# A hybrid decoder step on one core: w_in's columns in six pairs, with the delta rule's front and half its inverse between their tiles

## The chip, the cores and the metric

One core of a Trainium2 chip runs the whole program. The metric is the device time of one execution in microseconds (us). Below, PE is TensorE, DVE is VectorE, ACT is ScalarE, POOL is GpSimd, and SP is SyncE, which here only issues DMAs. All data is fp32. A fp32 weight product is made of three products of halves (a rounded part and its remainder), so every weight goes through a split first.

## What is computed

Two layers, D = 1024, over 256 prompt positions and 8 samples of one position each: 264 columns stand side by side everywhere. Each layer is

```python
x += 0.5 * post1(SwiGLU_1(pre1(x)))                  # 1024 -> 2816 -> 1024
x += post2(W_out concat[A, B, C, D](pre2(x)))        # heads fed by ONE input projection
x += 0.5 * post3(SwiGLU_2(pre3(x)))
# A dilated sliding-window attention   (q, k, v)      columns QA KA VA
# B forgetting attention, paged cache  (q, k, v, f)   columns QB VB KB, gates FB
# C gated delta rule                   (q, k, v, z, a, b)
#     q, k, v go through a 4-tap conv and SiLU; q, k are divided by their L2 norm per head
#     A_ij = (k_i beta_i) k_j exp(g_i - g_j), strictly lower;  T = inv(I + A)
#     v_new = T rhs;  out = q S + (q k^T * decay) v_new;  S = decay * S + k^T v_new
# D spatial gating                     (u, v)         columns UD VD
```

The 8 samples also attend to their own pasts: 8 pages of 128 cached positions each for B (read through a page table) and three windows for A, 11 tiles of 128x256 for the keys and 11 for the values of each sample. Each sample's delta state (16x1024) is read, updated and written.

## The kernel before, in words

There is no scheduler: each engine's program is written out by hand and runs in its order, and semaphores join them. A layer is six phases of weight products: gu1, dn1, wi (w_in), wo (w_out), gu2, dn2.

**Weights.** The weights of a phase come in pairs of tiles, s = 0 and 1, into two buffers. SP loads `raw`, ACT rounds it to `whi` (L591), DVE makes `wlo` = raw - whi (L888, helper `lo`), and PE runs three matmuls of 128x264 per 128 rows of the contraction (L1391, L1392, L1393, helper `three`). A wide tile is 256 columns: `wide_chunk` runs two halves of 24 matmuls, each into its own PSUM bank, and DVE scales them by the column norms into `proj` (helpers `take`, L985 to L1000). w_in has 7 pairs: six of 2 x 256 columns in the order of the matrix, and one narrow one for the rest.

**Between w_in and w_out.** PE turns `proj` to token-major (`tok`, `smp`) in 7 groups (L1504), then sums the gates with triangular constants (L1508 to L1513), turns the rows, builds decay terms from four-row operands (L1524, L1525), and runs the prompt's attention B (scores L1535, L1538, L1539; values L1566 to L1568), attention A, the spatial gating (L1644), and the delta rule: Gram products (L1657), transposes (L1665), and the triangular inverse in six levels, each a `y` product (L1678) and two products from it (L1687, L1688) with DVE work between (`lev`); after it new values (L1700), outputs (L1706) and the state (L1709). The conv of q, k, v is 7 tiles on DVE, each L1058 and three L1060.

**The samples.** SP reads the page table and issues each sample's keys into `kslot` (`keys`, L446, L435 to L437) and values into `vslot` (`vals`, L454). Samples use two slots in turn, so keys(b) waits until POOL used the slot (`k_used`), and vals(b) until PE did (`pv_mm`). POOL multiplies keys and queries (L855, L856, tile `prod`), DVE adds them up (L1114, L1116), ACT takes the exponent, and PE forms the values of two samples at a time (`sample_values`, L1590, L1592, four calls). The samples' own conv row `cv` is made on POOL and ACT, scaled on DVE (L1188, semaphore `s_conv`), and written to DRAM by SP (L513, `d_cn`), from where it comes back regrouped (`kq16`, `v64`) for the samples' delta state.

**The order that SP follows** after w_in's last matmul: keys and vals of samples 0 and 1 with the small stores between them, keys(2), keys(3), the gates' loads, eight output stores (L503 to L510), the wait for `s_conv` and L513, vals(2), vals(3), keys(4), keys(5), the eight loads of the states (L526), vals(4), vals(5), keys(6), keys(7), vals(6), vals(7). Page slots, `at_`, `qkt` and the other scratch lie in separate places of SBUF.

**The end of the stage.** `sample_values(3)`, the states' products, `so_mm` (L1733), DVE's normalisation of the samples' rows (L1340 to L1354), and PE's transposes of the mixed heads (L1740, L1741), behind which w_out's first matmul (L1391) stands.

## Time and profile before

| | us |
|---|---|
| median of 3 runs | 1602.6 (1593.21 to 1604.79) |
| the profiled execution | 1603.99 |
| its span | 1602.2 |
| w_in's last matmul starts, layer 0 | 314.73 |
| `s_conv` scale on DVE (L1188), layer 0 | 385.24 |
| last value page's issue, layer 0 | 483.01 |
| transposes of the mixed heads start, layer 0 | 546.62 |
| PE's mean granted clock over the span | 0.870 of 2.4 GHz |

How to read it: times of the trace count from the span's start. A row of the timeline is start, duration, engine, line, operation, output and inputs, shape and count, and in brackets how long the engine stood idle before it and on whom it waited. Rows with a count merge neighbours; their duration is from the first start to the last end. SPq is the queue that SP issues DMAs on, and its durations are those of issuing. Both layers run the same program, and layer 1 repeats layer 0 about 795 us later.

### The profile page before, as it was taken

What the parts mean: (1) busy time and instruction counts of PE and PEld (TensorE: products, weight loads), DVE (VectorE), ACT (ScalarE), POOL (GpSimd) and SP (SyncE); (2) the same over time, 40 slices, a digit from 0 to 9 for tenths busy, and PEclk for the clock granted to TensorE, in tenths of its full rate; (3) what the DMA queues carried; (4) which work ended last, traced back from release to release, by engine and by line L of the source; (5) the groups of instructions that cost most, each with busy time, mean ns of one, the idle gap of its engine ahead of it and who ended that gap; (6) DMA issues with size and microseconds to landing.
All of it is one profiled execution on the core that took longest, in us unless ns stands there. A gap on an engine that the chain in (4) does not pass through costs nothing.

```text
span 1602.2 us, 27946 instructions
## 1 busy us (share of the span) xinstructions
PE 1353.2 (84%) x9968; PEld 1257.8 (79%) x9968; DVE 944.8 (59%) x1508; ACT 652.6 (41%) x1054; POOL 216.7 (14%) x176
## 2 busy tenths in 40 slices
PE   6999979977587579999889999697866857699997
PEld 5999979966375369999889999697754735699996
DVE  4766355485654666664467654655756554666634
ACT  4655343343200255554456544434330004455543
POOL 1000010022332230000110000200323322200000
PEclk9999989967686589999989999899556966899998
DMA  6555554354461334555646556363444613255553
GB/s 213 183 184 160 163 177 131 96 155 138 147 192 49 93 105 134 184 172 162 182 129 190 172 155 181 106 199 97 129 130 138 185 38 106 83 184 183 159 168 94
DMA packets 286118, 234.15 MB, mean 146 GB/s; under 512 B 19898, under 2 KB 282018, under 8 KB 286056
## 3 DMA queue, kind: packets, MB, share of 16 engines
q1 hardware_dynamic: 286056, 233.37, 47.9%
q8 instruction: 33, 0.54, 0.1%
q14 instruction: 29, 0.24, 0.0%
HBM read 228.65 MB, written 5.37 MB: 146 GB/s over the span
## 4 chain that ended last, share of the span: by engine, by line
PE 76%; DVE 15%; ACT 3%; issue 3%; DMA 1%; SPq 0%; DVEq 0%; POOLq 0%; ACTq 0%
PE ps L1391 20%; PE ps L1392 19%; PE ps L1393 19%; PE ps L1590 2%; PE ps L1688 2%; DVE s L1114 2%; PE ps L1535 2%; DVE nlo L937 2%; PE ps L1687 1%; DVE yt L920 1%; PE ps L1538 1%; ACT whi L591 1%; PE ps L1504 1%; PE ps L1678 1%; PE ps L1733 1%
## 5 line engine op out<-in xcount | busy, mean ns | idle before, releaser
L1391 PE MATMUL ps<-nhi,whi 128*128 128x264 f32 x1936 | 564.2, 291 | 67.4 <-DVE nlo L937 47.0
L888 DVE TENSOR_TENSOR wlo<-raw,whi 128x1024 fp32r<-128x1024 f32 (+2 forms) x376 | 394.7, 1091 | 280.1 <-ACT whi L591 279.8
L1392 PE MATMUL ps<-nlo,whi 128*128 128x264 f32 x1936 | 558.5, 289 | 0.0
L1393 PE MATMUL ps<-nhi,wlo 128*128 128x264 f32 x1936 | 557.7, 288 | 0.0
L1391 PEld LDWEIGHTS ps<-nhi,whi 128*128 128x128 f32 x1936 | 375.2, 194 | 74.2 <-DVE nlo L937 35.9
L591 ACT ACTIVATE whi<-raw 128x1024 fp32r<-128x1024 f32 (+2 forms) x376 | 336.8, 945 | 190.9 <-PE ps L1393 113.4
L1392 PEld LDWEIGHTS ps<-nlo,whi 128*128 128x128 f32 x1936 | 375.4, 194 | 0.2
L1393 PEld LDWEIGHTS ps<-nhi,wlo 128*128 128x128 f32 x1936 | 373.2, 193 | 0.0
L1391 PE MATMUL ps<-hhi,whi 128*128 128x264 f32 x704 | 202.3, 287 | 9.1 <-DVE hlo L905 9.1
L1393 PE MATMUL ps<-hhi,wlo 128*128 128x264 f32 x704 | 201.4, 286 | 0.0
L1392 PE MATMUL ps<-hlo,whi 128*128 128x264 f32 x704 | 201.0, 286 | 0.0
L1391 PEld LDWEIGHTS ps<-hhi,whi 128*128 128x128 f32 x704 | 133.9, 190 | 9.9 <-issue 9.8
L1393 PEld LDWEIGHTS ps<-hhi,wlo 128*128 128x128 f32 x704 | 134.0, 190 | 0.0
L1392 PEld LDWEIGHTS ps<-hlo,whi 128*128 128x128 f32 x704 | 133.9, 190 | 0.0
L601 ACT ACTIVATE hhi<-h_t 128x264 f32 (+1 forms) x88 | 37.3, 424 | 172.7 <-DVE h_t L902 172.7
L813 POOL TENSOR_TENSOR ss_acc<-sq 128x264 f32<-128x264 f32 x12 | 10.0, 832 | 697.5 <-ACT sq L608 652.4
L816 POOL TENSOR_TENSOR ss_acc<-ss_acc,sq 128x264 f32<-128x264 f32 x72 | 60.8, 845 | 225.4 <-ACT sq L608 199.5
L855 POOL TENSOR_TENSOR prod<-kslot,q_bc 128x2048 f32<-128x2048 f32 x16 | 72.2, 4515 | 135.1 <-DVE s L1116 89.3
L905 DVE TENSOR_TENSOR hlo<-h_t,hhi 128x264 f32 (+1 forms) x88 | 38.2, 434 | 60.2 <-ACT hhi L601 60.2
L607 ACT ACTIVATE yt<-ps 128x264 f32 (+1 forms) x48 | 18.8, 391 | 92.9 <-PE ps L1393 92.9
L597 ACT ACTIVATE s_t<-s_t 128x264 f32<-128x264 f32 x88 | 36.3, 425 | 40.6 <-DVE s_t L895 40.3
L597 ACT ACT_TABLE_LOAD x40 | 51.3, 1283 | 0.7
(338 smaller groups left out, 1555.8 us busy)
## 6 DMA issues: line engine op xcount, KB each, us to landing
raw<-in_ffn_gate_dram SPq DMA_DIRECT2D x44, 1024.0 KB, 5.3
raw<-in_ffn_up_dram SPq DMA_DIRECT2D x44, 1024.0 KB, 5.4
raw<-in_ffn_down_dram SPq DMA_DIRECT2D x64, 704.0 KB, 4.5
raw<-in_w_in_dram SPq DMA_DIRECT2D x24, 1024.0 KB, 5.7
kslot<-in_cache_fox_k_dram SPq DMA_DIRECT2D x128, 128.0 KB, 2.7
vslot<-in_cache_fox_v_dram SPq DMA_DIRECT2D x128, 128.0 KB, 2.4
raw<-in_w_out_dram SPq DMA_DIRECT2D x8, 1024.0 KB, 5.1
kslot<-in_state_swa_k_dram SPq DMA_DIRECT2D x32, 128.0 KB, 2.7
```

What stands on the lines that cost most here:

```text
L591: act.activation(whi[s][:, a:b], raw[s][:, a:b], ACT.Copy).then_inc(S(f"w_hi{s}"), 1)
L597: act.activation(s_t[:, f, :], s_t[:, f, :], ACT.Silu).then_inc(S("silu"), 1)
L601: act.activation(hhi[:, bass.ds(2 * j + f, 1), :].rearrange("p o n -> p (o n)"), h_t[:, f, :], ACT.Copy).then_inc(S("h_hi"), 1)
L816: ins = tt_(ss_acc[:, :], ss_acc[:, :], sq8[:, t, :], ALU.add)
L855: tt_(prod[:, 0:NPG, :], kslot[:, i, 0:NPG, :], q_bc[:, i, GW:512].unsqueeze(1).broadcast_to([P, NPG, GW]), ALU.mult).then_inc(S("prod"), 1)
L888: tt2(wlo[s][:, a:b], raw[s][:, a:b], whi[s][:, a:b].bitcast(F32), ALU.subtract).then_inc(S(f"w_lo{s}"), 1)
L905: tt2(hlo[:, at, :].rearrange("p o n -> p (o n)"), h_t[:, f, :], hhi[:, at, :].rearrange("p o n -> p (o n)").bitcast(F32), ALU.subtract).t ...
L937: stt(nlo[:, t, :], x[:, t, :], gain(l + ahead, e, t), nhi[:, t, :].bitcast(F32), ALU.mult, ALU.subtract).then_inc(S("n_ready"), 1)
L1114: red(s13[:, u, 0:NPG, :], four_(prod[:, 0:NPG, :]), AX.X, ALU.add).then_inc(S("s_red"), 1)
L1391: mm(out, wh, hi_, start=first, stop=False)
L1392: mm(out, wh, lo_, start=False, stop=False)
L1393: return mm(out, wl, hi_, start=False, stop=last)
```

## The change

It does five things in each layer.

1. w_in's columns are regrouped into six pairs of wide tiles in the order C's q, k, v, then B's, A's, D's and z; the twelve gate columns come apart as a tile of 128x224 (`graw`), loaded by two DMAs of 4 and 8 columns a row, split by ACT and DVE, and multiplied in 24 matmuls ahead of pair 1. Wide matmuls: 24 tiles of 24 instead of 25.
2. After each half of pairs 1 to 5, PE runs a piece of what used to stand behind w_in: gates, sums, norms, decay broadcasts, Gram products, transposes, levels 0 to 2 of the inverse, and the token-major transposes. Levels 3 to 5 stand behind w_in, between attention B's pieces, and the new values, outputs and state of the delta rule stand between attention B and attention A.
3. The delta rule's front is rewritten: L2 norms and gates are added as logarithms and go in with one exponent; decays come from a broadcast and one DVE operation a head, written straight to `at_` and `qkt`; the conv of v's two tiles is on POOL (14 operations), that of q and k on DVE; POOL makes `wlo` for s = 1 of pairs 2 to 5.
4. The page slots `kslot` and `vslot` lie in the weight buffers; `at_`, `qkt`, `tt`, `tm`, `ys`, `kd` lie where `kslot` was, and `prod`, `q_bc` and others where `vslot` was. keys(0) waits for the last `wlo` of w_in, and all other pages for w_in's last matmul.
5. SP's order: keys(1), vals(0), vals(1), the eight output stores and the states' loads, then the wait for `s_conv`; keys(2) and keys(3) stand behind it. On DVE the `s_conv` scale stands behind the second new values of the delta rule. The samples' state work stands between the later samples' reductions instead of at the end.

```diff
+WCOL = ((QC, QC + GW), (QC + 2 * GW, QB_), (KB_, VB_), (QA, KA), (VA, VD), (UD, ZC))
...
+        w_at = here[0]
...
+        kslot = place("kslot", [P, 2, NKT, GW], at=w_at)
+        vslot = place("vslot", [P, 2, NKT, GW + 1], at=w_at + 8 * NKT * GW)
...
# SP
+                    for s in range(2):
+                        sp.wait_ge(S(f"w_lo{s}"), V(f"w_lo{s}", 2 * (P0["wi"] + WI_P)))
+                    keys(0)
...
                     for s in range(2):
                         sp.wait_ge(S(f"mm_done{s}"), V(f"mm_done{s}", M0["wo"]))
-                    sp.wait_ge(S("slot_zero"), V("slot_zero", 4))
-                    keys(0)
-                    vals(0)
...
-                    for b in (2, 3):
-                        keys(b)
...
                     sp.wait_ge(S("s_conv"), V("s_conv", 1))
                     sp.dma_start(d_cn.rearrange("c b (h e) -> (c b h) e", h=H), cv[:, 8, :]).then_inc(S("regroup"), 16)
+                    for b in (2, 3):
+                        keys(b)
...
# DVE
-                    sample_shift(0)
-                    dve.wait_ge(S("mix_r"), V("mix_r", 1))
-                    ts(cv[:, 8, :], cv[:, 8, :], small[0:96, 0:1], C("q_scale", 96), ALU.mult, ALU.mult).then_inc(S("s_conv"), 1)
...
+                    tt2(kb_n[:, 0, :], vb[:, 1, :], kb_n[:, 0, :], ALU.subtract).then_inc(S("rhs1"), 1)
+                    sample_shift(0)
+                    dve.wait_ge(S("vn_mm"), V("vn_mm", 2))
+                    dve.tensor_copy(vn[:, 1, :], ps[:, 5, 0:GW]).then_inc(S("vn"), 1)
+                    dve.wait_ge(S("mix_r"), V("mix_r", 1))
+                    ts(cv[:, 8, :], cv[:, 8, :], small[0:96, 0:1], C("q_scale", 96), ALU.mult, ALU.mult).then_inc(S("s_conv"), 1)
...
# PE
+                    def beside(j, s, i):
...
+                        elif (j, s, i) == (1, 1, 0):
+                            cumulate()
+                        elif (j, s, i) == (1, 1, 1):
+                            head_norms()
...
+                        elif (j, s) == (2, 1):
+                            broadcast(i)
+                        elif (j, s) == (3, 0):
+                            gram(i)
...
+                        elif (j, s, i) == (4, 1, 1):
+                            pe.wait_ge(S("tok_act"), V("tok_act", SMP_AT[3] + 1))
+                            level_z(0)
```

On PE the first of the new places is in w_in's second pair. Before, one half follows the other there; a stretch of the program before, at the end of w_in and into what follows it:

```order
L1393 MATMUL ps<-nhi,wlo_78 128x264
L1504 MATMUL ps<-const,proj 128x128 [waits pd_taken,pa_taken]
L1504 MATMUL ps<-const,proj 128x128 x7
...
L1504 MATMUL ps<-const,proj 8x128
L1508 MATMUL ps<-gate,const 128x8 [waits gate_act]
L1509 MATMUL ps<-gate,const 128x4
```

The program after, at the first half of pair 1's tile s = 1 (L1453 to L1455 are the three matmuls, L1573 to L1578 are L1508 to L1513 of before):

```order
L1455 MATMUL ps<-nhi,wlo_83 128x264
L1573 MATMUL ps<-gate,const 128x8 [waits gate_dve]
L1574 MATMUL ps<-gate,const 128x4
...
L1578 MATMUL ps<-gate,const 128x4
L1453 MATMUL ps<-nhi,whi_81 128x264 [waits pd_taken]
L1454 MATMUL ps<-nlo,whi_81 128x264
```

The gates' sums moved from behind all of w_in into the middle of its second pair, and the matmuls of the next half stand behind their wait.

On SP, around the wait for `s_conv`, before:

```order
L446 DMA kslot<-in_cache_fox_k_dram 128x256
L435 DMA kslot<-in_state_swa_k_dram 128x256
...
L501 DMA gb<-d_gate 32x2 [waits gb_pre]
...
L510 DMA out_swa_k_sample_dram<-smp 8x256
L513 DMA d_cn<-cv 96x64 [waits s_conv]
L454 DMA vslot<-in_cache_fox_v_dram 128x256 [waits pv_mm]
```

and after:

```order
L525 DMA out_swa_v_prompt_dram<-tok 128x2x256
L527 DMA proj<-in_state_gdn_s_dram 16x1024 x8
L531 DMA d_cn<-cv 96x64 [waits s_conv]
L470 TENSOR_LOAD ptab
...
L498 DMA q_bc<-d_q 128x512 [waits k_used0]
L486 ISA
L486 DMA kslot<-in_cache_fox_k_dram 128x256
```

Six samples' keys and values, instead of four samples' keys and six samples' values, stand behind that wait.

On DVE, ahead of the instruction that raises `s_conv`, before:

```order
L1101 COPY ptr<-ps 128x512 [waits p_turned]
L1103 RECIPROCAL small<-small 128x8 [waits p_exp]
L1105 TENSOR_TENSOR otok<-ps,small 128x2x256 [waits o_mm,dve_ch]
L1139 TENSOR_TENSOR s_119<-s_119,pmax_all 128x2x36 [waits s_max_all]
L1140 TENSOR_TENSOR s_119<-s_119,pmax_all 128x2x16
L1188 TENSOR_SCALAR cv<-cv,small,const 96x64 [waits mix_r]
```

and after, where `lf_turned`, `vn_mm`, `oc_mm` and `ks_mm` are raised by PE behind the inverse's levels and `scores(1)`'s matmuls:

```order
L1232 TENSOR_REDUCE s_124<-prod 128x12 [waits k_used0]
L1156 TENSOR_TENSOR tt<-tt,ps 128x4x64 [waits tm_act,z_mm0]
L1156 TENSOR_TENSOR tt<-tt,ps 128x4x64 [waits tm_act,z_mm1]
L1290 COPY ptr<-ps 128x256 [waits lf_turned]
...
L1232 TENSOR_REDUCE s_124<-prod 128x12 [waits k_used1]
L1296 COPY vn<-ps 128x256 [waits vn_mm]
...
L1318 TENSOR_TENSOR kb_n<-vb,kb_n 128x256
L1255 TENSOR_TENSOR s_124<-s_124,pmax_all 128x2x36 [waits s_max_all]
L1256 TENSOR_TENSOR s_124<-s_124,pmax_all 128x2x16
L1321 COPY vn<-ps 128x256 [waits vn_mm]
L1323 TENSOR_SCALAR cv<-cv,small,const 96x64 [waits mix_r]
```

The instruction that raises `s_conv` moved from behind attention B's first half to behind the whole inverse and both chunks' new values.

## Rows read from the trace of the kernel before

**Rows 1.** The page: the chain that ended last, by engine.

```profile
PE 76%; DVE 15%; ACT 3%; issue 3%; DMA 1%; SPq 0%; DVEq 0%; POOLq 0%; ACTq 0%
```

**Rows 2.** Windows: length; busy PE, PEld, DVE, ACT, POOL; PEclk, DMA share, GB/s.

```profile
252.00:315.10 63.10, 61.26 (x505) 60.97 (x504) 34.17 (x49) 19.54 (x22) 0.00 (x0) 1.00 0.46 144
...
330.00:385.50 55.50, 47.61 (x199) 39.87 (x200) 38.16 (x73) 19.14 (x43) 15.69 (x12) 0.59 0.50 153
385.50:483.50 98.00, 71.24 (x496) 55.64 (x495) 57.73 (x104) 14.28 (x34) 36.36 (x13) 0.74 0.53 160
```

**Rows 3.** Timeline of SP's queue, layer 0.

```profile
321.38 3.99 SPq L446 DMA_DIRECT2D kslot<-in_cache_fox_k_dram  x8
...
362.33 0.37 SPq L458 DMA_DIRECT2D q_bc<-d_q  x1
...
373.25 0.33 SPq L458 DMA_DIRECT2D q_bc<-d_q  x1
...
395.19 3.70 SPq L454 DMA_DIRECT2D vslot<-in_cache_fox_v_dram  x8
...
400.48 3.85 SPq L454 DMA_DIRECT2D vslot<-in_cache_fox_v_dram  x8
...
483.01 0.49 SPq L437 DMA_DIRECT2D vslot<-in_state_swa_v_dram  x1
```

**Rows 4.** Waits of SP's queue, both layers: total us, times, longest.

```profile
SPq L454 <- PE ps L1592: 17.5, 2, 9.0
```

**Rows 5.** Timeline: `s_conv` on DVE, and the end of the stage on PE.

```profile
385.24 0.30 DVE L1188 TENSOR_SCALAR cv<-cv,small,const 96x64 f32<-96x64 f32 x1
...
509.53 3.60 PE L1590 MATMUL ps<-vslot,s 128*4 128x257 f32 x28
...
531.55 6.43 PE L1733 MATMUL ps<-oms,const 100*8 100x256 f32 x16
546.62 0.66 PE L1740 MATMUL ps<-const,otok 128*128 128x128 f32 x2 [8.64 <-DVE smp_o L1354]
```

**Rows 6.** Timeline of PE: w_in's start and end, transposes, products of the inverse.

```profile
235.65 0.56 PE L1391 MATMUL ps<-nhi,whi 128*128 128x264 f32 x1 [7.49 <-DVE nlo L937]
...
236.23 0.42 PE L1393 MATMUL ps<-nhi,wlo 128*128 128x264 f32 x1
...
314.73 0.28 PE L1393 MATMUL ps<-nhi,wlo 128*128 128x264 f32 x1
315.53 8.41 PE L1504 MATMUL ps<-const,proj 128*128 128x128 f32 x75 [0.53 <-DVE proj L1000]
...
448.31 2.17 PE L1678 MATMUL ps<-tm,at__84 128*128 128x128 f32 x16
...
461.66 0.39 PE L1687 MATMUL ps<-ys,tt 128*128 128x128 f32 x2
461.89 0.39 PE L1688 MATMUL ps<-tt,ys 128*128 128x128 f32 x2
```

**Rows 7.** Timeline of ACT: the gates' chain.

```profile
325.32 0.23 ACT L676 ACTIVATE gate_t<-gate_in 128x36 f32<-128x36 f32 x1 [0.96 <-DVE gate_in L1017]
...
328.40 0.23 ACT L678 ACTIVATE gate_t<-gate_t 128x36 f32<-128x36 f32 x1
```

**Rows 8.** Timeline of DVE and POOL where a conv meets a product.

```profile
331.22 1.52 DVE L1060 SCALAR_TENSOR_TENSOR conv_t<-proj,cwt,conv_t 128x255 f32<-128x255 f32 x3
...
338.84 7.70 DVE L1060 SCALAR_TENSOR_TENSOR conv_t<-proj,cwt,conv_t 128x255 f32<-128x255 f32 x3
...
339.99 4.50 POOL L855 TENSOR_TENSOR prod<-kslot,q_bc 128x2048 f32<-128x2048 f32 x1
```

**Rows 9.** Timeline of PE: `scores(0)` from its first matmul to the next piece.

```profile
343.81 0.79 PE L1535 MATMUL ps<-proj 64*128 64x128 f32 x2
...
366.21 3.25 PE L1549 MATMUL ps<-const,conv_t 128*128 128x128 f32 x14
```

**Rows 10.** The page: DMA queue: packets, MB, share of 16 engines.

```profile
q1 hardware_dynamic: 286056, 233.37, 47.9%
```

More of the change, by code:

```diff
@@ L117, in constants @@
     put("eps", np.full((P, 1), EPS))
+    put("eps64", np.full((P, 1), HD * EPS))
+    put("half", (i[:, None] // HD == np.arange(2)[None, :]))
     scale = np.ones((P, 1))
@@ L243, in build @@
+        conv_t = place("conv_t", [P, NCT, L])
+        vb = place("vb", [P, 2, GW])
+        here[0] = max(here[0], f_at + 8 * FT * N + 16 * N)
         f_end = here[0]
@@ new lines, in _ @@
+                    h8 = lambda ap: ap.rearrange("p t (h i) -> p (t h) i", h=H)
+                    h22 = lambda ap: ap.rearrange("p (b a i) -> p a b i", b=2, a=2)
+                    four = lambda ap: ap.rearrange("p t (h d) -> p t h d", h=H)
+                    wide = lambda name: C(name).unsqueeze(1).broadcast_to([P, 8, P])
+                    for i in range(2):
+                        take(0, 0, i)
+                    lo("wi", 1, 0)
+                    for i in range(2):
+                        take(0, 1, i)
@@ new lines, in _ @@
+                    lo("wi", 1, 1)
+                    dve.wait_ge(S("gates_mm"), V("gates_mm", 1))
+                    tt2(proj[0:12, NPT - 1, :], ps[0:12, 4, 0:N], r_pre[0:12], ALU.mult).then_inc(S("gates_taken"), 1)
+                    dve.wait_ge(S("par_taken"), V("par_taken", 3))
+                    dve.wait_ge(S("pd_taken"), V("pd_taken", 4))
+                    for t in range(4):
+                        conv(t)
+                    for i in range(2):
+                        take(1, 0, i)
@@ new lines, in _ @@
+                    lo("wi", 2, 0)
+                    dve.wait_ge(S("gate_act"), V("gate_act", 1))
+                    ch(stt(gate[:, :, :], gate_in[:, :, :], 0.0, gate_t[:, :, :], ALU.max, ALU.add))
+                    tt2(gate[:, :, :], gate[:, :, :], mul12[:, :].unsqueeze(1).broadcast_to([P, 3, 12]), ALU.mult).then_inc(S("gate_dve"), 1)
+                    for i in range(2):
+                        take(1, 1, i)
+                    dve.wait_ge(S("gate_mm"), V("gate_mm", 1))
+                    dve.tensor_copy(cum[:, :], ps[:, 7, 40:64]).then_inc(S("cum_sb"), 1)
@@ new lines, in _ @@
+                    ch(stt(ex[:, :, 2, :], lk, -0.5, cg, ALU.mult, ALU.subtract))
+                    dve.tensor_copy(ex[:, :, 4, :], lnb)
+                    dve.tensor_copy(ex[:, :, 5, :], tot)
+                    tt2(ex[:, :, 0, :], ex[:, :, 0, :], lnb, ALU.add)
+                    tt2(ex[:, :, 3, :], ex[:, :, 2, :], tot, ALU.add).then_inc(S("ex"), 1)
+                    for i in range(2):
+                        take(2, 0, i)
+                    lo("wi", 3, 0)
+                    dve.wait_ge(S("gate_mm"), V("gate_mm", 2))
@@ new lines, in update @@
+                    def update(k):
+                        last = k == len(LEVELS) - 1
+                        part = lambda ap, side: ap.rearrange("p (c a e) -> p c a e", a=2, e=LEVELS[k])[:, :, side, :]
+                        for t in range(NT):
+                            dve.wait_ge(S(f"z_mm{t}"), V(f"z_mm{t}", k + 1))
+                            dve.wait_ge(S("tm_act"), V("tm_act", 2))
+                            if not last:
+                                tt2(part(tm[:, t, :], 0), part(tm[:, t, :], 0), part(ps[:, 4 + 2 * t, :], 0), ALU.subtract)
+                            tt2(part(tt[:, t, :], 1), part(tt[:, t, :], 1), part(ps[:, 5 + t if last else 5 + 2 * t, :], 1), ALU.subtract).then_inc(S(f"lev{t}"), 1)
@@ L1083, in _ @@
[L1083 to L1089 removed]
+                    masked_y(0)
@@ new lines, in level_z @@
+                    def level_z(k):
+                        last = k == len(LEVELS) - 1
+                        for t in range(NT):
+                            pe.wait_ge(S(f"ys{t}"), V(f"ys{t}", k + 1))
+                            for h in range(H):
+                                if not last:
+                                    mm(ps[:, 4 + 2 * t, hp(h)], tt[:, t, hp(h)], ys[:, t, hp(h)], start=True, stop=True)
+                                ins = mm(ps[:, 5 + t if last else 5 + 2 * t, hp(h)], ys[:, t, hp(h)], tt[:, t, hp(h)], start=True, stop=True)
+                            ins.then_inc(S(f"z_mm{t}"), 1)
```

1058 lines of the change are left out of this document (562 added, 496 removed).

## The prediction

> **What bounds the kernel now.** I read the page's chain first, then windows of the stretch that the change touches, then SP's queue in it, then single instructions. The chain is PE for 76% [rows 1], mostly weight products, and these the change leaves alone. The windows show two different halves [rows 2]. In w_in PE is busy 61.26 of 63.1 us at the full clock (505 matmuls, 0.121 each), with DVE at 34.17, ACT at 19.54 and POOL at nothing: there is room beside it on those engines, none on PE. Behind w_in PE is busy 71.24 of 98 us at 0.74, so something else leads there. It is SP's queue [rows 3]: keys of one sample follow those of another after 10.9 us (362.33 to 373.25), values after 5.3 (395.19 to 400.48), from 321.38 to 483.5. In that stretch it waits little: its longest wait is 9.0 us for `pv_mm` [rows 4], and `s_conv`, raised at 385.24 [rows 5], comes as SP reaches it. The end is PE again: `sample_values(3)` starts at 509.53, though its pages were issued by 483.5, and the transposes of the mixed heads start at 546.62 [rows 5]. I call w_in's end T_w (315.0 [rows 6]) and `s_conv`'s scale T_s (385.24 [rows 5], T_w + 70.2). From T_s to the transposes it is 161.4 us.
>
> **First part: w_in's stretch.** The wide matmuls are as many as before, 600 a layer. The pieces between them add to PE, at full clock: some 60 transposes at 0.112 (8.41 / 75 [rows 6]) 6.7; gates' sums 2.7 (L1508 to L1513, 330.21 to 332.9); Gram products 2.3 (L1657); the inverse's 8 transposes 0.9; three y levels at 2.2 and three z levels at 16 x 0.22 (461.66 to 461.89 [rows 6]) 3.6, 17.2; small ones 1.3. Sum 31. None of it is hidden: PE was full here.
>
> Then PE's in-order waits. The gates' sums stand in pair 1 and wait for the gates; behind them stands half of w_in. The gates need their matmuls, a transpose, ACT's chain of 3.3 us with two table loads (325.32 to 328.63 [rows 7]) behind a `whi` pair of 2, and a DVE step that stands behind the four convs of q and k, 4 x (0.35 + 1.52) = 7.4 [rows 8]. I schedule it: PE reaches the wait at 265.1, the gates come at 275.2: 10 us idle (bounds 3, if the convs finished early, and 12). The decay rows cost 2.9 by the same method, the first z level 1.8, other waits 1. Then the clock: after 7.49 us idle w_in's own third matmul takes 0.42 and not 0.28 [rows 6], and such matmuls start 0.22 apart for 4.6 us; that is 2 us. The narrow seventh pair and its waits go, -2. So T_w moves by 31 + 15.7 = 47, to 362. Bounds: +31 to +4 of waits (350), and 370.
>
> The gate columns' DMAs have packets of 16 and 32 bytes, 2048 a layer. A packet takes 0.479 x 16 x 1602 / 286056 = 43 ns [rows 10]; over 16 engines that is 5.5 us of queue beside gu1's weights, or nothing if it finds a gap. I take 0 (bounds 0 and 5.5).
>
> **Second part: from T_w to T_s.** Before, 70.2 us, in which `scores(0)` took 22.4 (343.81 to 366.21 [rows 9]) at half clock. Now DVE's `s_conv` scale stands behind the whole inverse, attention B's values and the second new values. In PE's order: z of level 2 3.6, y3 with its waits 2.9, transposes 1.8, z3 3.6, own samples' rows on DVE and y4 4.1, `scores(0)` 17.7 (between 22.4 at half clock and 11.2 at full; above the middle, since its four-row matmuls ran at half clock to the last [rows 9]), z4 5.7, the turn of q and k and y5 4.4, then DVE's mask, the reductions of the first sample and `lf_sb` 10.2, the decays' sums 4.6, new values 1.9, turn of p 2.0, outputs and state 2.6, values 4.5, the state's product 2.0, `scores(1)` 3.5, new values 1.9. Sum 77.0, so T_s = 439. Bounds: 57 with all of it at full clock and nothing blocked, 86 with all at half.
>
> In this sum 8 us are for one thing the trace shows: three convs' DVE operations that take 1.52 elsewhere take 7.70 when they meet POOL's 4.50-us product of keys [rows 8]. After the change products of samples 0 and 1 stand beside DVE's own-row work and `lf_sb`, on which PE waits: 3.2 + 5. The Trainium skill (SBUF — State Buffer, "Who interferes with whom") says that VectorE and GpSimd share a port pair, and that a VectorE operation with two SBUF inputs waits for a whole GpSimd instruction. By that rule, the trace agrees: the conv has two such inputs. The rule also speaks against putting v's conv and `wlo` on POOL beside DVE's convs in w_in's stretch; without it my sum would be 8 us a layer lower.
>
> **Third part: from T_s to the end.** SP has nothing to issue from about T_w + 35, when both slots are full, until T_s, since six samples stand behind the wait. Then it issues d_cn 0.4, keys(2, 3) 21.8, `kq16` and `v64` 3.5, vals(2, 3) 10.6, keys(4, 5) 21.6, vals(4, 5) 11.7, keys(6, 7) 21.0, a store 0.6, vals(6, 7) 12.0: 103.2 by the steps of [rows 3] (before, 98.3 from T_s with two waits of 9.0 and 3.4 in them and two samples' keys fewer). The last lands 2.7 later, and ACT's exponent for it stands behind the mix's norms: T_s + 109. Then `sample_values(3)` 6.6, its division 0.9, `so_mm` 6.4 [rows 5], and DVE's 8.6 [rows 5]: the transposes at T_s + 131. Before, 161.4: the samples' state chain (516.2 to 531.5) no longer stands behind `sample_values(3)`, and neither do the inverse and the new values, which held its start to 509.53. So this part gains 30.4. At full clock it is T_s + 126.
>
> **The sum.** A layer: +47 + 6.8 - 30.4 = +23.4. Two layers: +46.8. On the profiled execution, 1603.99, that makes 1650.8; the median of the runs lies 1.4 below, so 1649. What was hidden before (delta rule beside SP's pages) now stands in front of `s_conv`, which lets the pages go; that outweighs the shorter end.
>
> **Rivals.**
> *PE never idles (faster).* The place is the gates' sums: if DVE serves the gates before the convs end, the stall is 3 us or less, and a PE that does not idle keeps the full clock that w_in has in [rows 2] through the levels and `scores(0)`. Then T_w = 350, T_s = 407, transposes 533: -13.6 a layer, -27.2 in all, 1575. Against it: DVE's order puts the convs ahead, and the clock stayed at 0.59 through the four-row matmuls [rows 2], which remain. It decides for faster once T_s comes before 416 in layer 0. Chance 0.13.
> *Stall as forecast, then full clock (no change).* T_w 362, T_s 362 + 57 to 65, end +126: 545 to 553 against 546.6, -1.6 to +6.4 a layer, 1599 to 1615. For it: behind w_in there is now denser PE work than before. Chance 0.15.
> *More of the same (slower still).* POOL's 14 conv operations and 8 `wlo` halt DVE in w_in, T_w 362 to 370; at half clock T_s is 84 to 86 later and the transposes 132 behind that: 578 to 588, +31 to +41 a layer, 1665 to 1684. For it: a DVE operation of 0.48 became one of 6.6 in [rows 8]. Chance 0.25, and the packets of the gates' DMAs are in it.
> *The change does not do what it says*, since the pieces stand between the tiles but hide nothing, PE being full there: that is the forecast's own ground, and has no chance of its own.
>
> **How the numbers follow.** The forecast itself, 1620 to 1664, holds 0.47. The range must leave out 2 in 10: its low end is 1595, which lets out most of the first rival; its high end 1690, above the third. A measurement of this kernel tells about 1% from no change (its runs spread by 0.7%), 1586.6 to 1618.6. Faster 0.13; within 1% 0.15; slower 0.72.
>
> **What would show it.** In the trace after: w_in's last matmul near 362 in layer 0 (350 to 370), with one idle of some 10 us before L1573; a PEclk under 0.8 in the 77 us behind it; no page issued in the 35 to 40 us before `s_conv` at about 439; a `sample_values(3)` some 109 us behind that, bound by its pages; the mixed heads' transposes 5 to 10 us nearer to the last page. Wrong if T_s comes before 416, if PE does not wait at L1573, or if DVE shows no operation stretched by a POOL product.

## The result, and the profile after

The kernel after takes 1700.98 us (median of 4 runs, 1699.47 to 1702.37), the kernel before 1600.32 beside it (1593.21 to 1604.79): a ratio of 1.0635, interval 1.060 to 1.067. The forecast was 1649.0, range 1595 to 1690. The direction was right, the size was not: the time lies above the range, 52 us over the forecast. The profiled execution took 1702.08, its span 1700.3. Medians and ratios are those of fast runs: one execution below, 2044.35 us at a granted clock of 0.62 in the squares' run, was slow and is left out.

The page's chain that ended last (shares of the span of 1700.3 us):

```profile
PE 64%; DVE 13%; SPq 9%; issue 7%; ACT 4%; DMA 1%; POOL 1%; POOLq 0%; DVEq 0%; ACTq 0%
```

Against [rows 1], PE's share of the chain fell from 76% to 64%. SP's queue, which stood at 0%, has 9% now, and "issue", time in which an engine waited for nothing that the profile shows, went from 3% to 7%. Those two entries are where to look.

Windows of layer 0 (length; busy PE, PEld, DVE, ACT, POOL with instructions; granted clock, DMA share, GB/s). They are cut at w_in's end, at `scores(0)`, at `s_conv`, at the last pages, and at the transposes of the mixed heads:

```profile
250.00:367.80 117.80, 102.08 (x749) 97.50 (x749) 56.17 (x126) 40.18 (x55) 34.50 (x29) 0.88 0.27 79
367.80:385.00 17.20, 11.74 (x100) 11.11 (x99) 12.18 (x18) 4.38 (x8) 7.83 (x8) 0.95 0.50 150
385.00:410.60 25.60, 25.60 (x89) 20.00 (x87) 1.87 (x5) 0.00 (x0) 0.00 (x0) 0.50 0.59 177
410.60:451.60 41.00, 31.19 (x203) 29.22 (x202) 23.25 (x40) 13.38 (x29) 6.85 (x3) 0.75 0.00 1
451.60:558.00 106.40, 32.89 (x228) 18.44 (x228) 51.39 (x83) 9.84 (x26) 38.95 (x15) 0.60 0.58 172
558.00:598.40 40.40, 12.25 (x68) 3.44 (x68) 9.85 (x18) 9.00 (x12) 13.65 (x8) 0.58 0.20 66
```

Read the last column first. From 410.6 to 451.6 the DMA engines carry 1 GB/s: nothing is in the queue. From 451.6 to 558 they carry 172, and PE is busy 32.89 of 106.4 us: it mostly waits for the samples' pages and what hangs on them. From 558 to 598.4 neither is busy, and no engine passes 14 of 40 us: a chain of short steps. Before, [rows 2] has PE busy 71.24 of 98 us in the stretch with the pages.

The three places are in the timelines. SP's queue (start, duration, line, operation), where "x8" are the eight pages of one sample:

```profile
400.07 3.73 SPq L527 DMA_DIRECT2D proj<-in_state_gdn_s_dram  x8
...
451.94 0.31 SPq L531 DMA_DIRECT2D d_cn<-cv  x1
...
457.46 4.36 SPq L486 DMA_DIRECT2D kslot<-in_cache_fox_k_dram  x8
...
548.90 3.95 SPq L494 DMA_DIRECT2D vslot<-in_cache_fox_v_dram  x8
```

The queue stands idle from 403.8 to 451.9, 48.1 us, as long as `s_conv` isn't raised (DVE's scale is at 451.62). PE, at the places where it waits or changes its pace:

```profile
273.29 0.59 PE L1573 MATMUL ps<-gate,const 128*128 128x8 f32 x2 [9.81 <-DVE gate L1081]
...
367.71 0.28 PE L1455 MATMUL ps<-nhi,wlo 128*128 128x264 f32 x1
...
384.50 3.75 PE L1656 MATMUL ps<-tm,at__88 128*128 128x128 f32 x16 [4.52 <-DVE tt L1156]
...
429.60 1.22 PE L1807 MATMUL ps<-ptr,const 128*128 128x256 f32 x2 [6.55 <-DVE ptr L1291]
...
576.57 3.60 PE L1780 MATMUL ps<-vslot,s 128*4 128x257 f32 x28 [42.85 <-ACT s L764]
...
598.44 0.66 PE L1878 MATMUL ps<-const,otok 128*128 128x128 f32 x2 [8.64 <-DVE smp_o L1416]
```

So T_w is 367.8 instead of 315.0 (+52.8), T_s is 451.6 instead of 385.24, and the transposes start at 598.44 instead of 546.62 [rows 5]: +51.8 in this layer. The last piece of the chain, read in order of time, holds the largest single surprise (start, length, engine, tile, line):

```profile
557.39 0.39 POOL pmax_all L906
...
557.87 11.58 issue
569.44 1.88 POOL tm L915
571.33 1.87 POOL tt L915
...
573.22 1.23 DVE small L1396
...
574.47 0.32 ACT small L781
...
576.11 0.23 ACT small L782
576.34 0.19 ACT s L764
```

POOL's all-reduce for the last two samples is done at 557.8, and DVE has the exponent's input ready at 558.15. The exponent (L764) runs at 576.3. On ACT it stands behind the mixed heads' norms (L781, L782), which need DVE's reductions (L1396) of squares that POOL makes (L915), and POOL begins them 11.6 us after its all-reduce.

### The profile page after: what moved, and what is told of

Same layout as the page of the kernel before. It is cut to its first block, busy times and chain, and to the rows that moved or that the text cites. A ratio compares the mean times of both kernels' runs of the same rounds, so it can differ in the third digit from the quotient of the medians.

```text
span 1700.3 us, 27532 instructions
## 1 busy us (share of the span) xinstructions
PE 1335.2 (79%) x9902; PEld 1238.7 (73%) x9902; DVE 898.9 (53%) x1450; ACT 656.4 (39%) x1048; POOL 275.5 (16%) x219
## 4 chain that ended last, share of the span: by engine, by line
PE 64%; DVE 13%; SPq 9%; issue 7%; ACT 4%; DMA 1%; POOL 1%; POOLq 0%; DVEq 0%; ACTq 0%
PE ps L1453 17%; PE ps L1454 17%; PE ps L1455 17%; SPq L470 2%; SPq L486 2%; DVE wlo L938 2%; ACT whi L605 2%; SPq L494 2%; DVE nlo L987 1%; PE ps L1735 1%; PE ps L1656 1%; DVE yt L970 1%; PE ps L1665 1%; PE ps L1738 1%; PE ps L1666 1%
## 5 line engine op out<-in xcount | busy, mean ns | idle before, releaser
L1453 PE MATMUL ps<-nhi,whi 128*128 128x264 f32 x1920 | 569.1, 296 | 63.5 <-DVE nlo L987 46.4
L1455 PE MATMUL ps<-nhi,wlo 128*128 128x264 f32 x1920 | 559.2, 291 | 0.0
L938 DVE TENSOR_TENSOR wlo<-raw,whi 128x1024 fp32r<-128x1024 f32 (+1 forms) x352 | 373.9, 1104 | 295.0 <-ACT whi L605 295.0
L1453 PEld LDWEIGHTS ps<-nhi,whi 128*128 128x128 f32 x1920 | 379.0, 197 | 72.8 <-DVE nlo L987 34.2
L605 ACT ACTIVATE whi<-raw 128x1024 fp32r<-128x1024 f32 (+1 forms) x368 | 333.8, 956 | 169.7 <-PE ps L1455 102.7
L1454 PEld LDWEIGHTS ps<-nlo,whi 128*128 128x128 f32 x1920 | 379.2, 197 | 0.2
L1455 PEld LDWEIGHTS ps<-nhi,wlo 128*128 128x128 f32 x1920 | 376.5, 196 | 0.0
L1453 PE MATMUL ps<-hhi,whi 128*128 128x264 f32 x704 | 201.1, 286 | 9.1 <-DVE hlo L955 9.1
L1455 PE MATMUL ps<-hhi,wlo 128*128 128x264 f32 x704 | 200.0, 284 | 0.0
L1453 PEld LDWEIGHTS ps<-hhi,whi 128*128 128x128 f32 x704 | 132.4, 188 | 10.2 <-issue 9.9
L1455 PEld LDWEIGHTS ps<-hhi,wlo 128*128 128x128 f32 x704 | 132.7, 188 | 0.0
L1780 PE MATMUL ps<-vslot,s 128*4 128x257 f32 x352 | 46.6, 546 | 107.3 <-ACT s L764 107.3
L1780 PEld LDWEIGHTS ps<-vslot,s 128*4 128x4 f32 x352 | 13.6, 107 | 135.1 <-ACT s L764 107.9
L1230 DVE TENSOR_REDUCE s<-prod 128x32 f32<-128x2048 f32 x16 | 36.5, 2281 | 85.9 <-POOL prod L902 85.9
```

The lines of the kernel that those rows point to most:

```text
L605: act.activation(whi[s][:, a:b], raw[s][:, a:b], ACT.Copy).then_inc(S(f"w_hi{s}"), 1)
L938: tt2(wlo[s][:, a:b], raw[s][:, a:b], whi[s][:, a:b].bitcast(F32), ALU.subtract).then_inc(S(f"w_lo{s}"), 1)
L1230: red(s13[:, u, 0:NPG, :], four_(prod[:, 0:NPG, :]), AX.X, ALU.add).then_inc(S("s_red"), 1)
L1453: mm(out, wh, hi_, start=first, stop=False)
L1454: mm(out, wh, lo_, start=False, stop=False)
L1455: return mm(out, wl, hi_, start=False, stop=last)
```

## The experiments

The theory after reading the trace: orders make the loss, and three of them hold PE (pages behind `s_conv`, the last exponent behind the squares, the gates' sums in w_in). The rival: a length of work that no order takes away (w_in's pieces, SP's pages, the half clock). Each run is compared with the kernel before; the kernel after stands at 1.0635. "A layer" is half the difference in ratio, at 1600 us. All but one are variants of the kernel after, and their line numbers differ from its own by up to three.

**The last exponent first.**

```diff
# ACT
                     sample_exp(2)
+                    sample_exp(3)
                     act.wait_ge(S("mix_ss"), V("mix_ss", 3))
...
-                    sample_exp(3)
```

> The changed kernel, with ACT's exponent for the last two samples (sample_exp(3)) put ahead of the mixing norms' Ln and Exp instead of behind them. Theory: in the changed kernel the last value product waits 42.85 us for that exponent, of which 18 us (558.2, when DVE has its input ready, to 576.2) are only ACT's order; with the order undone the product starts near 559, and then the mixing on POOL, which ends at 586.6, becomes the last one: transposes at about 588 instead of 598.4, 10 us a layer, 1701 - 21 = 1680 us. Rival (the last pages bind there): the order is covered and nothing moves, 1701.

1694.74, ratio 1.0601 (1.0565 to 1.0636), 3 us a layer; the interval overlaps that of the kernel after. In the profiled execution, the fastest of the four, the transposes start at 592.34, 6.1 sooner. PE at the end of the stage:

```profile
558.16 3.59 PE L1780 MATMUL ps<-vslot,s 128*4 128x257 f32 x28 [24.90 <-ACT s L764]
...
574.95 6.53 PE L1871 MATMUL ps<-oms,const 100*8 100x256 f32 x16 [7.76 <-DVE oms L1265]
```

`sample_values(3)` did start 18.4 us sooner (558.16 for 576.57), as expected. But its division on DVE (L1263 to L1265) stands behind the same reductions of the squares, so a part of the gain went back into a wait of PE for `oms` (7.76), and another into the one for `smp_o` (10.86 for 8.64). One wait was hidden behind another for the same release.

**The squares ahead of the last all-reduce.**

```diff
# POOL, sample 7
                         tt_(prod[...], kslot[...], ...).then_inc(S(f"k_used{i}"), 1)
+                        if b == B - 1:
+                            for t in range(NT): tt_(squares[t], otok[:, t, :], otok[:, t, :], ALU.mult).then_inc(S("o_sq"), 1)
                         if i == 1:
                             pool.partition_all_reduce(...)
```

> The changed kernel, with POOL's two squares of the mixed heads put ahead of its last all-reduce instead of behind it (they need nothing of it); ACT and DVE as changed. In the changed kernel POOL starts them 11.7 us after that all-reduce has ended, with nothing that the profile shows to wait for, and with the exponent put ahead the end came only 6 us a layer earlier, because DVE's last division stood behind the same squares. Theory (the 11.7 us follow every all-reduce on POOL and stand in the chain of the last samples): the squares run before 556, the exponent follows at 563 instead of 576, transposes 11 to 13 us a layer earlier, 1701 - 24 = 1677; the gap then shows ahead of the mixing (L920) instead. Rival (the gap belongs to the squares' inputs): it moves with them, under 4 us a layer.

1680.26 (3 runs), ratio 1.0554 (1.0505 to 1.0602), 6.5 us a layer, where 12 were expected; the transposes start at 589.19, 9.2 sooner. On POOL:

```profile
552.05 1.89 POOL L911 TENSOR_TENSOR tm<-otok 128x1024 f32<-128x1024 f32 x1
...
561.96 0.39 POOL L914 PARTITION_ALL_REDUCE pmax_all<-pmax  x1 [6.17 <-issue]
571.18 1.89 POOL L921 TENSOR_TENSOR otok<-otok,small 128x1024 f32<-128x1024 f32 x1 [8.83 <-issue]
```

The squares now follow the product without a gap. The idle time did not go with them: it stands ahead of what comes after the all-reduce, here the mixing (L921). ACT gave the mixing its norm at 566.88, so of the 8.83 us the last 4.3 have no input to wait for. So idle time follows the all-reduce and not the squares; that all 11.6 us of the kernel after belong to it is not shown. The all-reduce itself started 4.6 us later, with the squares ahead of it.

**Keys 2 and 3 ahead of the wait for `s_conv`.**

```diff
# SP
+                    for b in (2, 3):
+                        keys(b)
                     sp.wait_ge(S("s_conv"), V("s_conv", 1))
                     sp.dma_start(d_cn..., cv[:, 8, :])
-                    for b in (2, 3):
-                        keys(b)
```

> The changed kernel, with keys(2) and keys(3) issued by SP ahead of the wait for s_conv, as the kernel before did. Theory (SP stands idle from 404 to 452 while it has pages to issue): keys(2) goes at 404, keys(3) after k_used1 at 431, and behind s_conv stand 22 us less; the next wait is pv_mm for vals(2), near 460, so about 16 us a layer come off the last page, 1701 - 32 = 1669. Rival (the pages did not bind, or POOL's product of sample 2 now halts DVE ahead of s_conv): under 8 us a layer, over 1685.

1669.24, ratio 1.0440 (1.0393 to 1.0486), 15.6 us a layer, as expected. SP's queue and the transposes:

```profile
410.35 4.34 SPq L486 DMA_DIRECT2D kslot<-in_cache_fox_k_dram  x8
...
433.07 4.02 SPq L486 DMA_DIRECT2D kslot<-in_cache_fox_k_dram  x8
...
462.96 3.68 SPq L494 DMA_DIRECT2D vslot<-in_cache_fox_v_dram  x8
```

```profile
582.55 0.66 PE L1878 MATMUL ps<-const,otok 128*128 128x128 f32 x2 [8.64 <-DVE smp_o L1416]
```

Keys 2 go out 47 us sooner, but keys 3 only when POOL has used its slot, and vals 2 only when `sample_values(0)` has (462.96 for 477.36). Of 20 us of keys taken off the end (457.46 to vals 2 at 477.36), 15.9 are gained.

**`s_conv` itself early.**

```diff
# DVE: squares of cv behind update(3), the scale ahead of update(4)
                     update(3)
+                    ch(tt2(cv[0:64, 7, :], cv[0:64, 8, :], cv[0:64, 8, :], ALU.mult))
+                    red(small[0:64, 0:1], cv[0:64, 7, :], AX.X, ALU.add).then_inc(S("mix_ss"), 1)
...
+                    ts(cv[:, 8, :], cv[:, 8, :], small[0:96, 0:1], C("q_scale", 96), ALU.mult, ALU.mult).then_inc(S("s_conv"), 1)
                     update(4)
# ACT: the two small activations between ahead of the copies of q and k
```

> The changed kernel, with the samples' conv norm and scale made early: DVE's squares behind level 3's update, ACT's Ln and Exp behind the gates' SiLU, DVE's scale (s_conv) ahead of level 4's update; SP's order as changed. Theory (s_conv's place holds the pages): s_conv comes near 390 instead of 452, SP then issues keys(2) at 404 and keys(3) after k_used1 at 431, vals(2) after pv_mm near 460: the same 16 us a layer as with the keys ahead of the wait, 1669. If the wait for s_conv were only one of several that end together, under 5 us a layer, over 1690.

1666.32, ratio 1.0407 (1.0373 to 1.0441), 18 us a layer. The scale ran at 391.66, and the rest follows the run above to within 2 us:

```profile
405.80 0.42 SPq L531 DMA_DIRECT2D d_cn<-cv  x1
...
464.45 3.68 SPq L494 DMA_DIRECT2D vslot<-in_cache_fox_v_dram  x8
```

Two different edits, one in SP's order and one in DVE's, give the same time within their intervals. So it is keys 2 and 3 behind `s_conv` that cost, and once these are free, the values of samples 0 and 1 lead.

**The gates' sums half a tile later.**

```diff
# PE
-                        elif (j, s, i) == (1, 1, 0):
-                            cumulate()
                         elif (j, s, i) == (1, 1, 1):
+                            cumulate()
                             head_norms()
```

> The changed kernel, with the gates' cumulative sums on PE moved one half of a tile later (behind the second half of pair 1's s = 1 instead of the first). Theory: of PE's 9.8 us of waiting for the gates 5.8 are then filled with 24 matmuls, and the half clock behind the wait gets shorter: 6 to 8 us a layer off the end of w_in, and as much off the end, 1701 - 14 = 1687. Rival (what comes off there is given back behind w_in, where SP and POOL set the pace): under 2 us a layer, over 1697.

1694.23, ratio 1.0580 (1.0548 to 1.0613), 4.4 us a layer, with an interval that overlaps that of the kernel after.

```profile
274.80 0.60 PE L1573 MATMUL ps<-gate,const 128*128 128x8 f32 x2 [6.89 <-DVE gate L1081]
```

The wait fell by 2.9 us to 6.89, where 4 were expected to be left of it. w_in ended 1.8 sooner (365.88), but `s_conv` came at 451.82, no sooner than before the edit: from 433 to 447 the granted clock was 0.62 here and 0.74 in the kernel after, with PE busy 12.6 of 14 us in both. PE still was 1.7 us ahead at `lf_sb`'s products (427.90 for 429.60), so what was won in w_in was lost behind them, and the clock is what the rows show to differ there. The transposes did start 2.6 sooner.

**All five orders, then the samples' sums too.** The first run has the five edits above together. The second also puts `sample_add(0)` and `sample_add(1)`, DVE's sums of products, ahead of `update(4)` on DVE.

> The changed kernel with the orders put right together: s_conv early, keys(2) and keys(3) ahead of its wait, the squares ahead of the last all-reduce, the last exponent ahead of the norms, the gates' sums half a tile later. Theory (pages 14.5 us a layer, the last exponent 12, the sums 1 to 2, and they add up): 28 us a layer, 1701 - 56 = 1645. Rival (they cover each other): as the better of them alone, 1666. Neither reaches 1600: w_in's end, 52 us later than before, and the pages behind it stay.

> As the run with all orders, and DVE's reductions of samples 0 and 1 moved from behind the mask of attention B into DVE's 25 us of idle time beside scores(0), which lets POOL make sample 1's product there instead of beside lf_sb. Theory (in the changed kernel POOL's product at 424.8 halted DVE's L1291 for 4.04 us, PE waited 6.55, and two reductions of 3.2 stood ahead of it): the first value product comes 8 to 10 us a layer earlier, and with it vals(2), which wait for it: 1645 - 17 = 1628. Rival (SP's own pace): under 3 us a layer, over 1639.

1640.91, ratio 1.0291 (1.0262 to 1.0320), and 1619.16, ratio 1.0166 (1.0130 to 1.0203). The five single gains, with `s_conv` counted once, add up to 0.0034 + 0.0081 + 0.0228 + 0.0055 = 0.040; together they gave 0.0344. Each of these ratios is known to some 0.0035, so the sum and the run agree, and whether the exponent and the squares cover each other is not shown. The sums of the samples are worth 10 us a layer: they release POOL's product of the next key pair and with it PE's wait for `ptr` (6.55), which fell to 1.17. Still 1.7% above the kernel before, with all three orders of the theory undone, so they were not the whole.

**POOL's product behind level 3.** On top of the last kernel, POOL's first product waits until DVE has done level 3.

```diff
# POOL
                         if b:
                             pool.wait_ge(S("s_red"), V("s_red", 2 * b))
+                        else:
+                            for u in range(NT):
+                                pool.wait_ge(S(f"lev{u}"), V(f"lev{u}", 4))
                         tt_(prod[:, 0:NPG, :], ...
```

> As the run with the samples' sums early, and POOL's product of sample 0 waits for level 3 of the inverse, so that it no longer stands beside DVE's own-row work (L1273 took 3.93 us there, and PE waited 4.6 for level 3). Two theories of the half clock in scores(0), 0.50 for 25 us: (a) PE's 4.6 us of waiting just ahead lowers it; then without that wait scores(0) takes 11 to 13 us instead of 22.4, and 3.5 + 10 us a layer come off: 1619 - 27 = 1592. (b) The four-row and 64-row matmuls of scores(0) themselves keep it low: then only the wait goes, 3 to 4 us a layer: 1619 - 7 = 1612, with scores(0) still at 22 us or falling to it after its first us.

1601.66 (10 runs), ratio 1.0018 (0.9990 to 1.0047): 12 us a layer more, and the time of the kernel before. PE goes into `scores(0)` without the wait of 4.5 us and at the full clock, and then:

```profile
377.86 2.02 PE L1659 MATMUL ps<-tm,at__88 128*128 128x128 f32 x16 [0.94 <-DVE tt L1160]
379.81 0.48 PE L1737 MATMUL ps<-proj 64*128 64x128 f32 x2
...
382.96 0.48 PE L1737 MATMUL ps<-proj 64*128 64x128 f32 x2
...
384.17 0.79 PE L1737 MATMUL ps<-proj 64*128 64x128 f32 x2
```

A group of six matmuls (two on 64 rows, four on 4) takes 1.05 us three times (379.81 to 382.96), once 1.21, then 1.87 (384.17 to 386.04) eight times. No idle time stands between; in a window from 384.2 to 399.1 PE is busy all of 14.9 us at a granted clock of 0.50. The full clock fell while PE was busy throughout, in matmuls on 64 and on 4 rows. `scores(0)` took 19.3 us, and from 399.1 to 430 the clock was 0.92. The transposes of the mixed heads start at 546.56; before, 546.62 [rows 5].

Not all of this gain is the product beside DVE's own-row work. PE reaches the product behind `lf_sb` at 413.57 for 421.18, 7.6 us sooner. Another 4.5 us come at the end of the stage, where the edit did nothing but shift the times: in the 1.0166 kernel (1614.47 in its profile) DVE's squares of the samples' rows (L1408) ran beside POOL's mixing, took 1.83, 2.08 and 2.11 us, and PE waited 13.18 for `smp_o`; here the mixing ends before them, they take 0.68, 0.40 and 0.40, and the wait is 8.64.

```profile
545.94 1.83 DVE L1408 TENSOR_TENSOR ptr<-smp_o 8x512 f32<-8x512 f32 x1
...
558.36 0.66 PE L1877 MATMUL ps<-const,otok 128*128 128x128 f32 x2 [13.18 <-DVE smp_o L1416]
```

In layer 1 the wait fell from 12.76 to 8.76, but the matmuls ahead of it took 2.9 us longer, and the profiled layer as a whole gained nothing (the transposes there start 11.05 sooner, 11.8 of it from layer 0). So a part of the 12 us is luck in how two engines' times fall.

**Without the four-row matmuls.** The same kernel but the one before this (1.0166), with the four-row matmuls of `scores(0)` left out; the forget terms of attention B are not computed.

```diff
# PE
-                                ins = mm(o, qh[...], kh[...], start=True, stop=(m == 1))
-                                if m == 0:
-                                    mm(o, rows[:, 0, ...], hr(h), start=False, stop=False)
-                                    ins = mm(o, hr(h), rows[:, 1, ...], start=False, stop=True)
+                                ins = mm(o, qh[...], kh[...], start=True, stop=True)
```

> As the run with the samples' sums early, but scores(0) leaves out its 24 four-row matmuls of 36 (the forget gates' terms are missing from attention B of the prompt, so this is a measurement and no variant). By (b) of the run before this one, if the four-row matmuls hold the clock down, the 12 left run at full clock after a few us: under 2.5 us in all, 20 us a layer. If 64-row matmuls hold it too, they take 7.5 us (12 of 36 at the same rate), 15 us a layer. The end gains less than that where SP's pages set the pace: vals(2) wait for the first value product, so 12 to 15 us of it should show a layer: 1619 - 27 = 1592.

1596.29 (10 runs), ratio 0.9988 (0.9962 to 1.0014), 14 us a layer where `scores(0)` fell from 22.4 to 2.70:

```profile
384.32 2.70 PE L1734 MATMUL ps<-proj 64*128 64x128 f32 x24
...
398.23 1.94 PE L1789 MATMUL ps<-const,tok 128*128 128x128 f32 x8 [7.45 <-DVE tt L1157]
```

The granted clock is 0.50 at their start (384.3 to 385.0), 0.53 to 386.0, and 1.00 from there, so the 24 matmuls on 64 rows did not keep it down. Nor is the clock the whole price. The 24 on 64 rows of `scores(1)`, with nothing between them, take 3.46 us at 0.50 in this run, and 1.92 in the run before:

```profile
421.00 3.46 PE L1734 MATMUL ps<-proj 64*128 64x128 f32 x24
```

At the same half clock `scores(0)` with its 48 on 4 rows between them takes 22.4 us, and two matmuls on 64 rows there take 0.72 us from start to start (0.36 each for 0.144). At the full clock its twelve groups, at 1.05 each, would be 12.6 (an estimate). So the clock is worth some 10 us of the 22.4, and the four-row matmuls with what they do to their neighbours some 11 even at the full clock; why a neighbour gets slower stays open. Part of what is won comes back as a wait of 7.45 for DVE, whose sums of sample 1 now stand ahead of level 4 and wait for POOL's product.

**The remainders of the weights back on DVE.** The 1.0166 kernel with `wlo` for s = 1 on DVE and not on POOL.

```diff
# POOL
-                    for j in range(2, WI_P):
-                        lo("wi", j, 1)
# DVE, between the pieces of w_in
+                    lo("wi", 2, 1)
...
```

> As the run with the samples' sums early, with the weights' remainders (wlo) of s = 1, pairs 2 to 5, made by DVE again and not by POOL (2.35 us a pair instead of 4.7, and no POOL reads beside DVE there; in the changed kernel DVE's L1092 took 2.00 and L938 2.88 beside POOL). Theory: DVE has 62 us of idle time in w_in's 118, the remainders come 2 to 4 us sooner, nothing is gained or lost where PE did not wait for them: within 3 us of 1619. Rival (POOL was taken for this with reason): DVE's rows, masks and levels come later and PE waits, over 2 us a layer: over 1624.

1619.43, ratio 1.0166 (1.0098 to 1.0235): no difference. From 250 to 367.8 DVE is busy 64.14 us and POOL 16.05, where the kernel after has 56.17 and 34.50. w_in ended at 369.20 and not at 364.73, and the transposes at 564.61 and not at 558.36; but in layer 1 the transposes start 3.9 sooner (1345.84 for 1349.77), so no gain or loss of the order shows. The interval leaves room for some 6 us a layer either way: POOL's part in w_in is not where the 50 us a layer went.

**The kernel before, with the samples' state work between.** One idea of the change by itself, in another place: the states' steps leave the end of the stage and stand between levels 3 to 5 and the new values. In the kernel after they stand between the later samples' reductions (L1373 to L1390). All else is as before.

```diff
# DVE, kernel before
+                    beside = {3: decayed, 4: summed, 5: differed}
...
+                        if k in beside:
+                            beside[k]()
...
-                    ch(ts(state[:, :, :], state[:, :, :], eb[:, 0:1], None, ALU.mult))
-                    ch(tt2(sk, state[:, :, :], kc16, ALU.mult))
-                    red(sk_r[:, :], sk.rearrange("p k v -> p v k"), AX.X, ALU.add).then_inc(S("sk"), 1)
# PE: the first state product behind level 4, the second behind ks_mm; ACT: sg ahead of sample_exp(3)
```

> The kernel before, with one thing of the change alone: the samples' state update is no longer done behind the last value product, but its DVE steps one by one between the inverse's levels 3 to 5 and the new values, its two sums on PE there too (skp and sk_r lie in free places of proj). Theory (in the kernel before 15.3 us of that chain stand behind sample_values(3), and DVE idles beside each level): 8 to 13 us a layer, 1600 - 21 = 1579. Rival (the steps lie on the chain of the levels, which sets sample_values(3)): within 4 us a layer of 1600, or above it.

1574.45 (6 runs, 1569.25 to 1586.14), ratio 0.9877 (0.9841 to 0.9914): 10 us a layer, and faster than both kernels. Its end of the stage on PE, against [rows 5]:

```profile
520.14 3.62 PE L1746 MATMUL ps<-oms,const 100*8 100x256 f32 x16 [0.98 <-DVE oms L1149]
537.61 0.66 PE L1753 MATMUL ps<-const,otok 128*128 128x128 f32 x2 [13.86 <-DVE smp_o L1363]
```

`so_mm` starts 11.4 us sooner, the transposes 9.0. The wait for `smp_o` is 13.86 instead of 8.64, and DVE and POOL of that stretch say why:

```profile
524.51 2.24 DVE L1355 TENSOR_TENSOR ptr<-smp_o 8x512 f32<-8x512 f32 x1
...
532.43 2.92 DVE L1361 TENSOR_TENSOR smp_o<-smp_o,small 8x1024 f32<-8x1024 f32 x1 [1.90 <-ACT small L764]
```

```profile
524.31 1.90 POOL L870 TENSOR_TENSOR otok<-otok,small 128x1024 f32<-128x1024 f32 x1 [7.26 <-ACT small L757]
```

DVE's normalisation of the samples' rows now meets POOL's mixing: 2.24 us for an operation that took 0.68 in the kernel before, 2.92 for one that took 1.21. It is the collision of the 1.0166 kernel again.

## Why the prediction was wrong in size

**The first part, w_in: +52.8, forecast +47.** The idle time at L1573 is 9.81 (said 10), and the waits from 250 on 15.7, as forecast. Added up from their starts, the pieces take 31.5 us (said 31). The step that failed is the clock: "w_in's own third matmul takes 0.42 ... that is 2 us". The 600 matmuls on weights, the gates' 24 with them, take 85.4 us from w_in's start, and before 75.7: 9.7 more, not 2. (w_in also starts 1.1 us sooner, which hides a part; the sums are good to about 1 us.) Such matmuls start 0.22 apart and not 0.12 in four places behind the gates: behind the wait to 281, at 284 to 288, and behind each of the two broadcasts with four-row operands (L1611), 302 to 305 and 308 to 311, the last of them with no idle time ahead. The forecast had priced one such place. The granted clock was 0.56 to 282, 0.88 to 296, 0.69 to 310, and 0.99 only from there:

```profile
273.20:282.00 8.80, 8.00 (x37) 7.83 (x37) 0.90 (x4) 1.98 (x3) 5.41 (x7) 0.56 0.40 121
...
296.00:310.00 14.00, 12.04 (x49) 10.17 (x50) 6.63 (x22) 3.63 (x4) 2.52 (x2) 0.69 0.26 76
310.00:367.80 57.80, 55.22 (x457) 53.65 (x457) 25.59 (x57) 14.88 (x20) 13.82 (x12) 0.99 0.24 70
```

**The second part, T_w to T_s: +83.8, forecast +77.0 (before, 70.2).** The step that failed is "`scores(0)` 17.7", a middle between 22.4 and 11.2. It took 22.4, from 388.18 to 410.58, all of it at 0.50 (in layer 1 it took 20.0, its first three groups at the pace of the full clock). The run with the product moved makes 17.7 look out of reach: even entered at the full clock with no idle time, `scores(0)` takes 19.3. [rows 9] had the right price, and I moved away from it towards a clock that no row showed in these matmuls. That is 4.7 of the 6.8 us. The blocks of DVE by POOL's product were of the size forecast: the waits are 4.52 and 6.55 (forecast 3.2 and 5; in the repaired kernels 0.94 and 1.17 are left of them without a block). Some 1 to 2 us of this part stay without a row of their own. On DVE:

```profile
376.94 3.93 DVE L1273 TENSOR_SCALAR small<-small 8x8 f32<-8x8 f32 x1
...
425.50 4.04 DVE L1291 TENSOR_TENSOR ptr<-const,gate 8x256 f32<-8x256 f32 x1
```

POOL's products of 4.60 and 4.51 us start at 376.25 and 424.76. The second row has two inputs in SBUF, as the rule that the prediction cited wants, and takes 0.40 where no product stands beside it. The first, on 8x8 elements, has one, and takes 0.16 elsewhere. The Trainium skill (SBUF — State Buffer, "Who interferes with whom") also says that copies and `tensor_scalar` can enter modes that take both ports and then contend with GpSimd. The trace agrees in time, with 3.93 us for 64 elements, though no row shows the mode.

**The third part, T_s to the transposes: 146.8, forecast 131.** This is over half of the miss. SP's pages took 102.4 us behind T_s by the trace (forecast 103.2), and the exponent's input was ready at T_s + 106.5 (forecast + 109). The step that failed is the sentence "ACT's exponent for it stands behind the mix's norms: T_s + 109": I named the wait and priced it at the 3 us between 103.2 + 2.7 and 109. The wait is worth 18: 11.6 on POOL behind the all-reduce, 3.8 of squares, 1.2 of DVE's reduction, 1.8 of ACT. From the exponent to the transposes it was 22.2, as forecast (22). Before, POOL's idle time behind the last all-reduce (491.74 to 501.60) lay under a wait for `st_s`, so nothing showed that it had to be there. Two other rows of before did show such a time, behind the all-reduces at 379.99 and 418.14, and I didn't look for what "issue" on POOL stood for:

```profile
387.31 4.52 POOL L855 TENSOR_TENSOR prod<-kslot,q_bc 128x2048 f32<-128x2048 f32 x1 [6.85 <-issue]
...
426.87 4.50 POOL L855 TENSOR_TENSOR prod<-kslot,q_bc 128x2048 f32<-128x2048 f32 x1 [8.33 <-issue]
...
501.60 1.90 POOL L863 TENSOR_TENSOR tm<-otok 128x1024 f32<-128x1024 f32 x1 [9.46 <-DVE st_s L1293]
```

One reading of before was half the truth as well: `s_conv` "comes as SP reaches it" holds in layer 0; in layer 1 SP waited 8.5 us for it.

**The sum.** Misses of 5.8, 6.8 and 15.8 make 28.4 a layer: 51.8 for a forecast of 23.4. Twice that is 57, and the median came out 52 above the forecast.

**The rivals.** "PE never idles" failed at its condition (the wait was 9.81). "Then full clock" failed at `scores(0)`. "More of the same" had the right sign and the right places (`T_w` 362 to 370, T_s 84 later) but for the third part 132 and not 147, so that it ended at 1684. No rival held the POOL order at the end, and the range was too narrow for that.

**What the whole comes to.** The ground of the forecast was right: PE was full in w_in, and work put there is paid in full. Every kernel after keeps w_in's end some 50 us late; with these orders mended the transposes stand at 546.56 against 546.62. So the work that moved, with all that stayed of the change, only paid for itself, and edits of order alone took back the 100 us. The steps from run to run, in ratio, are 0.0228 for the pages behind `s_conv`, 0.0116 for the exponent, the squares and the gates' sums (what is left of the five orders' 0.0344), 0.0125 for the samples' sums, and 0.0148 for POOL's product beside DVE, of which a part is the collision at the end of the stage. These sum to 0.0617, all but 0.0018 of the loss, as steps of one chain must; each depends on those ahead of it. Moving the states' work off the end of the stage is good by itself: some 20 us in the kernel before, in the place between the levels. What the change's own place for it is worth no run shows alone.

## What to carry to other kernels

When work moves in front of an instruction that lets DMAs go, price the idle queue behind it, and hoist that instruction (and the transfers that don't need it) first. Filling gaps on an engine that has none only moves its end. For every wait that you can name in another engine's program, write the whole chain to its releaser with prices, even if it was hidden before; a gain is real only when the second waiter for the same release is gone too. After each edit that shifts times, look again at which operations of DVE now run beside POOL's.

## What the runs showed that I had not expected

- POOL stands idle on both sides of each all-reduce with nothing shown that it waits for: 6.1 to 6.4 us ahead of it (489.01, 526.00, 557.39) and 7 to 12 behind it, before the next ordinary operation (11.66 in the kernel after, 11.70, 8.83, 7.71 in others). The Trainium skill (GPSIMD Engine Reference, "2.1 Instruction dispatch") names some 6 us for the first call to freshly loaded code, with no instruction to be seen. The idle time ahead of the all-reduce is of that size; no row shows code being loaded there. The part behind it stayed behind the all-reduce when the squares went ahead. Why it is 7 us at one place and 12 at another stays open.
- The granted clock falls to 0.50 (1.2 of 2.4 GHz) in matmuls on 4 and 64 rows that follow each other without idle time (384.17 above), and stays there to their end; it rises from 0.50 to 1.00 at 386.0 in the 24 on 64 rows alone. And 24 on 64 rows with nothing between them take 3.46 us at 0.50, where with 48 on 4 rows between them it is 22.4.
- An operation of DVE on 64 elements can take 3.93 us, where a product of POOL stands beside it, and 0.16 where none does. The same kind of meeting, DVE's rows of the samples beside POOL's mixing, costs 4.5 and 5.2 us a layer in two of these kernels (waits of 13.18 and 13.86 for 8.64).
